# Sparse attention's first loads and query scaling placed in the selection stage, its first masks on VectorE, and the softmax combination of differential attention in pieces of 512 keys

## The reference

```
# sparse ("nsa") attention, 8 heads in 2 groups; compressed, selected and window branches
imp = where(forced, 1e9, p_cmp @ a_sel); _, idx = top_k(imp, 8)     # 8 blocks of 64 keys for each query and group
s = q . k_selected * scale ; p_sel = softmax(s - slope * dist)      # selected branch
s = q . k_window   * scale ; p_win = softmax(s - slope * dist)      # window branch, 512 keys
out = g0 * o_cmp + g1 * o_sel + g2 * o_win

# differential attention, 4 heads, two score maps each
p = softmax(q_c . k_c * scale - slope * dist)        # c = 0, 1; causal, up to 2048 keys
a = p[0] - lam * p[1]
out = a @ v
```

## Time and profile before

| | us |
|---|---|
| median of 3 runs | 3420.95 |
| lowest and highest | 3409.36, 3424.22 |
| the profiled execution's own time | 3418.37 |
| its span in the trace | 3416.6 |

### The profile page before, as it was taken

One profiled execution on the slowest core, in us unless ns is written; L12 is line 12 of the kernel. 1 busy time (PEld: TensorE's weight loads), 2 busy tenths in 40 slices (PEclk: granted clock), 3 DMA queues, 4 the chain that ended last, 5 costly groups with the idle time before them and its releaser, 6 DMA issues. The chain is left out here.

```text
span 3416.6 us, 37491 instructions
## 1 busy us (share of the span) xinstructions
PE 2990.3 (88%) x13210; PEld 1767.3 (52%) x13211; DVE 1345.3 (39%) x3149; ACT 1000.7 (29%) x2050; POOL 558.6 (16%) x568
## 2 busy tenths in 40 slices
PE   8999999999977758989999969999699899859990
PEld 5644444444446635555665646666544355547670
DVE  3421212111114545555565647777511111152236
ACT  1100000000005524545555536666411012113332
POOL 0121110111003330221222120000121100001116
PEclk9999999999988769999999979999899999969995
DMA  3211211121141220011111020110254333615848
GB/s 118 77 63 68 71 66 57 68 71 65 59 143 47 80 84 27 15 51 35 55 41 49 7 93 1 38 38 1 111 219 144 143 129 123 270 60 208 319 166 307
DMA packets 120754, 323.41 MB, mean 95 GB/s; under 512 B 13216, under 2 KB 49696, under 8 KB 112416
## 3 DMA queue, kind: packets, MB, share of 16 engines
q1 hardware_dynamic: 100320, 247.54, 20.5%
q0 software_dynamic: 14096, 51.39, 4.6%
q10 hardware_dynamic: 6192, 22.55, 1.6%
HBM read 206.42 MB, written 115.02 MB: 94 GB/s over the span
## 5 line engine op out<-in xcount | busy, mean ns | idle before, releaser
L305 PE MATMUL p_ps<-token_sums,p_ws 128*128 128x512 f32 x768 | 340.0, 592 | 0.0
L305 PEld LDWEIGHTS p_ps<-token_sums,p_ws 128*128 128x128 f32 x768 | 145.9, 190 | 183.8 <-issue 183.8
L305 PE MATMUL p_ps<-xnT,p_w 128*128 128x512 f32 x512 | 233.1, 598 | 5.2 <-PEq L59 5.2
L1683 PE MATMUL o_ps<-o_w,o_mT 128*128 128x512 f32 x512 | 224.2, 596 | 14.0 <-DMA o_w<-in_w_out 14.0
L314 ACT ACTIVATE p_kept<-p_ps 128x512 f32<-128x512 f32 x32 | 19.1, 598 | 737.4 <-PE p_ps L305 737.4
L1038 PE MATMUL b_po<-b_probT,vsw 128*64 128x256 f32 (+1 forms) x1824 | 231.1, 375 | 0.0
L1113 DVE CUSTOM_DVE_ANT_0 b_prob_s<-b_pq,b_sel 128x896 f32<-128x896 f32 (+5 forms) x192 | 167.8, 911 | 144.0 <-PE b_pq L997 124.4
L327 DVE TENSOR_TENSOR p_kept<-p_ps,p_kept 128x512 f32<-128x512 f32 x96 | 66.4, 692 | 391.6 <-PE p_ps L305 391.6
L1275 PE MATMUL d_pq<-d_keys,d_q 64*128 64x512 f32 (+3 forms) x640 | 177.7, 589 | 27.4 <-DVE d_seg_max L1381 15.1
L1381 DVE CUSTOM_DVE_ANT_0 d_prob<-d_pq,d_bias 128x1024 f32<-128x1024 f32 (+6 forms) x192 | 167.5, 910 | 72.7 <-PE d_pq L1275 70.2
L997 PE MATMUL b_pq<-ks,b_q 64*128 64x512 f32 (+3 forms) x688 | 166.0, 542 | 29.0 <-DVE b_seg_max L1113 16.1
(11 more groups left out here) (277 smaller groups left out, 4755.9 us busy)
## 6 DMA issues: line engine op xcount, KB each, us to landing
projT<-p_stage SPq DMA_DIRECT2D x128, 256.0 KB, 2.3
y<-e_y ACTq DMA_DIRECT2D x43, 512.0 KB, 4.3
p_w<-in_wt SPq DMA_DIRECT2D x16, 1024.0 KB, 5.5
gates_T<-projT SPq DMA_DIRECT2D x16, 1024.0 KB, 9.9
wgu<-in_w_gu SPq DMA_DIRECT2D x4, 4096.0 KB, 15.7
y<-m_zeros POOLq DMA_DIRECT2D x20, 512.0 KB, 11.8
p_xin<-in_x SPq DMA_DIRECT2D x16, 512.0 KB, 3.7
mergedT<-m_stage SPq DMA_DIRECT2D x8, 1024.0 KB, 11.4
```

Source lines behind the costliest of these rows:

```text
L305: mm = nc.tensor.matmul(ps[n % 8][:], weights[:, k, :], moving[:, k, :], start=(k == 0), stop=(k == HK - 1))
L1683: mm = nc.tensor.matmul(ps[b][k][:], mT[:, b, dt, :], w[:, dt, k * 512:(k + 1) * 512], start=(dt == 0), stop=(dt == DT - 1))
```

## The change

In the selection stage SyncE also issues, behind the store of `ya`, the query scales, queries and distances of pairs 0 and 1 and the window distances, and GpSimd scales the queries of pairs 0 and 1. The tiles for these move to a scope that begins before the compression stages. In sparse attention the masks of pair 0 are added by VectorE, at the head of its list, and those of pair 1 by GpSimd, at the head of its own. In differential attention `combine` issues one instruction for each chunk of up to 512 keys, and `turn` waits for its own chunk. Cut diff:

```diff
@@ selection
             sp.dma_start(d["ya"], s.ya[:]).then_inc(ya_out, 16)
+            sp.dma_start(s.b_qscale[:], d["nsa_qscale"]).then_inc(s.b_const_in, 16)
+            for k in range(2):
+                load_queries(sp, d, s, k)
+            for k in range(2):
+                load_distances(sp, d, s, k)
+            sp.dma_start(s.b_wdist[:], d["win_dist"]).then_inc(s.b_const_in, 16)
             sp.wait_ge(ya_out, 16)
+
+        @block.gpsimd
+        def _(pool):
+            pool.wait_ge(s.b_const_in, 32)
+            for k in range(2):
+                scale_queries(nc, pool, s, k)
+def load_queries(sp, d, s, k):
+    p = PAIR_ORDER[k]
+    sp.dma_start(s.b_q[k % 2][:], d["qkT"][0:PAIRS, :, p * 2 * P:(p + 1) * 2 * P].rearrange("i p c -> p i c")).then_inc(s.b_q_in[k % 2], 16)
+def load_distances(sp, d, s, k):
+    for j in range(2):
+        n = (2 * PAIR_ORDER[k] + j + 1) * P
+        for g in range(GROUPS):
+            sp.dma_start(s.b_sel[:, j, g, sel_at(k):sel_at(k) + n], d["dist"][:, T - n:T]).then_inc(s.b_dist_in[k % 2], 16)
+def scale_queries(nc, pool, s, k):
+    pool.wait_ge(s.b_q_in[k % 2], 16 * (k // 2 + 1))
+    for i in range(PAIRS):
+        x = s.b_q[k % 2][:, i, :]
+        nc.gpsimd.tensor_scalar(x, x, s.b_qscale[:, i:i + 1], None, mybir.AluOpType.mult).then_inc(s.b_q_ready, 1)
@@ sparse_attention
+        def mask_row(eng, op, k, j, g, done):
+            t = 2 * PAIR_ORDER[k] + j
+            n = 2 * (t + 1)
+            x = sel[:, j, g, sel_at(k):sel_at(k) + (t + 1) * P].rearrange("p (b c) -> p b c", c=SEL_BLOCK)
+            op(x, x, s.mask[:, g, t, 0:n].unsqueeze(2).to_broadcast([P, n, SEL_BLOCK]), ALU.add).then_inc(done, 1)
...
-            sp.dma_start(qscale[:], d["nsa_qscale"]).then_inc(const_in, 16)
-            sp.dma_start(wdist[:], d["win_dist"]).then_inc(const_in, 16)
             load(0)
             load(1)
...
-            pool.wait_ge(const_in, 32)
-            scale_queries(0)
-            mask(0)
             mask(1)
-            scale_queries(1)
             make_rates(0)
...
-            pe.wait_ge(const_in, 32)
...
-                    if branch == "S" and i == 0:
-                        dve.wait_ge(masked, 4 * (u // PAIRS + 1))
+                    if branch == "S" and u < PAIRS:
+                        dve.wait_ge(first_masked, 4)
+                    elif branch == "S" and i == 0:
+                        dve.wait_ge(masked, 4 * (u // PAIRS))
...
-            dve.wait_ge(const_in, 32)
+            dve.wait_ge(dist_in[0], 64)
+            for j in range(2):
+                for g in range(GROUPS):
+                    mask_row(dve, nc.vector.tensor_tensor, 0, j, g, first_masked)
+            dve.wait_ge(s.b_const_in, 32)
@@ differential_attention
-                if f == f_first[u]:
-                    pe.wait_ge(combined, u + 1)
+                pe.wait_ge(combined, f + 1)
...
-                        dve.wait_ge(combined, u - 2)
+                        dve.wait_ge(combined, f_end[u - 3])
...
-                nc.vector.scalar_tensor_tensor(out=prob[0][u % 4][:, 0:n], in0=prob[1][u % 3][:, 0:n], scalar=stat[:, u % RING, 6:7],
-                                               in1=prob[0][u % 4][:, 0:n], op0=ALU.mult, op1=ALU.add).then_inc(combined, 1)
+                for f in range(f_first[u], f_end[u]):
+                    cols = slice(flat[f][1], flat[f][1] + flat[f][2])
+                    nc.vector.scalar_tensor_tensor(out=prob[0][u % 4][:, cols], in0=prob[1][u % 3][:, cols], scalar=stat[:, u % RING, 6:7],
+                                                   in1=prob[0][u % 4][:, cols], op0=ALU.mult, op1=ALU.add).then_inc(combined, 1)
```

More of the change, by code:

```diff
@@ L722, in _, with sel_at @@
                 nc.vector.tensor_scalar(s.mask[:, g], imp[:, g], NEG, NEG, ALU.not_equal, ALU.mult)
+SELW = 20 * P
+def sel_at(k):
+    return 0 if k % 2 == 0 else SELW - (2 * PAIR_ORDER[k] + 2) * P
+def load_queries(sp, d, s, k):
[7 more added lines that the diff above has]
+def scale_queries(nc, pool, s, k):
+    from concourse import mybir
+    pool.wait_ge(s.b_q_in[k % 2], 16 * (k // 2 + 1))
+    for i in range(PAIRS):
+        x = s.b_q[k % 2][:, i, :]
+        nc.gpsimd.tensor_scalar(x, x, s.b_qscale[:, i:i + 1], None, mybir.AluOpType.mult).then_inc(s.b_q_ready, 1)
 def chunks_of(start, count):
@@ L852, in sparse_attention @@
         sb = lambda name, shape: ctx.enter_context(nc.sbuf_tensor("b_" + name, shape, fp32))
-        wdist = sb("wdist", [P, WINDOW + P])
-        q = [sb(f"q{b}", [P, PAIRS, 2 * P]) for b in range(2)]
-        qscale = sb("qscale", [P, PAIRS])
+        wdist, q, sel, dist_in, q_ready = s.b_wdist, s.b_q, s.b_sel, s.b_dist_in, s.b_q_ready
         ya = [sb(f"ya{b}", [P, 2, NSA_HEADS * HD]) for b in range(2)]
-        sel = sb("sel", [P, 2, GROUPS, SELW])
         prob_s = [sb(f"prob_s{k}", [P, GROUPS, T]) for k in range(4)]
@@ L899, in load @@
                     sp.wait_ge(q_ready, PAIRS * (k - 1))
-                sp.dma_start(q[b][:], d["qkT"][0:PAIRS, :, cols].rearrange("i p c -> p i c")).then_inc(q_in[b], 16)
-                if k >= 2:
+                    load_queries(sp, d, s, k)
                     sp.wait_ge(scaled, GROUPS * (last_seg[(last_unit[k - 2], "S")] + 1))
[L903 to L906, removed]
+                    load_distances(sp, d, s, k)
                 if k >= 2:
@@ L928, in _ @@
         def _(pool):
[L929 to L933, removed]
             def mask(k):
-                p, b = PAIR_ORDER[k], k % 2
-                pool.wait_ge(dist_in[b], 64 * (k // 2 + 1))
+                pool.wait_ge(dist_in[k % 2], 64 * (k // 2 + 1))
                 for j in range(2):
-                    t = 2 * p + j
-                    n = 2 * (t + 1)
                     for g in range(GROUPS):
-                        x = sel[:, j, g, room(k):room(k) + (t + 1) * P].rearrange("p (b c) -> p b c", c=SEL_BLOCK)
-                        nc.gpsimd.tensor_tensor(x, x, s.mask[:, g, t, 0:n].unsqueeze(2).to_broadcast([P, n, SEL_BLOCK]), ALU.add).then_inc(masked, 1)
+                        mask_row(pool, nc.gpsimd.tensor_tensor, k, j, g, masked)
             def make_rates(u):
@@ L2281, in program @@
                 s.gates = sb(nsa, "gates", [P, NT, 3 * NSA_HEADS])
+                s.b_q = [sb(nsa, f"b_q{b}", [P, PAIRS, 2 * P]) for b in range(2)]
+                s.b_sel = sb(nsa, "b_sel", [P, 2, GROUPS, SELW])
+                s.b_wdist = sb(nsa, "b_wdist", [P, WINDOW + P])
+                s.b_qscale = sb(nsa, "b_qscale", [P, PAIRS])
+                s.b_q_in = [nc.alloc_semaphore(f"b_q_in{b}") for b in range(2)]
+                s.b_dist_in = [nc.alloc_semaphore(f"b_dist_in{b}") for b in range(2)]
+                s.b_const_in, s.b_q_ready = nc.alloc_semaphore("b_const_in"), nc.alloc_semaphore("b_q_ready")
                 with ExitStack() as cmp:
```

18 lines of the change are left out of this document (5 added, 13 removed).

## The result

The changed kernel takes 3402.21 us (median of 17 runs, 3396.3 to 3409.95), the kernel before beside it 3420.95 (17 runs, 3409.36 to 3426.86). The ratio is 0.9945, 95% interval 0.9937 to 0.9953: 18.7 us faster, where 38 were forecast. Half of the forecast is missing, and it is missing in one place.

The account below looks back on a forecast made before the run. TensorE, busy 88% of the span, was taken as the bound, so its idle time counts. 3418.4 - 13.9 (opening) - 22.4 (differential attention) = 3382.1, stated as 3383 us; range for 8 in 10: 3367 to 3407.

Parts of the forecast that it names:

- First masks on VectorE: Start of sparse attention: VectorE's four masks take 1.2 us, first score at 1212.5 instead of 1216.74, 4.3 us gained.
- rival 1: Start of sparse attention: VectorE's and GpSimd's masks take turns; 3392.5 if VectorE begins, 3396 if GpSimd begins; chance 0.33.
- the opening: Selection and start of sparse attention: first score 4.3 us earlier and a 9.6 us wait gone, together 13.9 us.
- Loads and scaling: Selection: loads behind the store land at 1203.5, GpSimd scales until 1210.8, so sparse attention starts at 1211.1 instead of 1205.96.
- Pair 1's masks and the wait at the turn: Sparse attention: GpSimd's masks run 1211.1 to 1225.0, so TensorE's 9.62 us wait for unit 0's rates goes whole.
- Combination in pieces: Differential attention: earlier turns gain 17.4 us over four heads, 0.14 us per extra piece; 22.4 us with the clock.
- clock term: Differential attention: shorter TensorE idle times spare part of the loss to a lower clock, 5 us, bounded by 0 and 13.
- rival 2: Differential attention: TensorE arrives earlier only to wait for `scale`; gain some 3 us, time 3401.5; chance 0.12.
- rival 3: Differential attention: turns gain nothing, 96 extra pieces cost 0.219 us each on VectorE's path, 21 us longer, 3425.5; chance 0.05.

Follow-up runs that it names:

- constants early: The changed kernel with the window distances loaded ahead of the queries and distances instead of behind them; 3390.57 us, ratio 0.9915.
- GpSimd behind: The changed kernel with one wait more: GpSimd starts pair 1's masks only when VectorE's four are done; 3384.66 us, ratio 0.9893.
- The opening with both faults mended: The changed kernel with window distances loaded early and GpSimd's masks waiting for VectorE's four; 3380.63 us, ratio 0.9877.
- the opening alone: The changed kernel with the combination whole again, so only loads, query scaling and first masks are moved; 3423.89 us, ratio 1.0005.
- late turn: The changed kernel, pieces kept, but TensorE's first turn of a unit waits for its last piece; 3433.96 us, ratio 1.0034.
- two pieces: The changed kernel with each combination in at most two instructions, the first 512 keys and then the rest; 3399.9 us, ratio 0.9935.
- second pair first: The changed kernel with window distances loaded early, pair 1's distances loaded ahead of pair 0's, and no wait between the engines' masks; 3389.78 us, ratio 0.991.

## Why the prediction was half right

- **The step that failed is "First masks on VectorE"**, which took 1.2 us for the four masks. They took 14.46, because rival 1 held, in its second form: GpSimd first, one of its masks ahead of each of VectorE's. That form had the turn of the rates back at its old time and the opening giving nothing. It was priced at 3396 from the earlier trace rows, whose overlapping pairs showed each engine waiting for the other; the argument against it, that four short instructions without a wait among them would run in one go, is what the single masks above refute. Of the 16.5 us by which the first score came late (1229.00 for 1212.5) the turns are 13.3.
- **Loads and scaling.** The other 3.2: scaling began at 1206.82 for 1203.5, 0.9 of it because the whole execution was later there. The bytes were counted right, but the slow start of the loads was not hidden under the store: from 1188 to 1190, just behind it, the DMA moved 102 GB/s. SyncE took 10.72 us to issue the eight distance loads while the 4 MB store was under way, the load issued last, for which GpSimd waits, went out at 1191.70, and it took 15.0 us to land. With the constants early, GpSimd began at 1194.28 and the stage was 7.5 us shorter. The prediction noted that GpSimd waits for that load and never asked whether an order without the wait was at hand.
- **Pair 1's masks and the wait at the turn.** Right. From first score to turn it is 1245.22 - 1216.74 = 28.5 us before, 19.05 after and 19.07 with GpSimd behind: the 9.62 us wait is gone whole. The time does not show it, because the first score itself comes 12.3 us later.
- **The opening with both faults mended** gives 21.7 us in medians, for 13.9 forecast. In its trace the turn of the rates stands 51.1 us behind the selection's first load, for 70.1 before: 19.0 us, which is the forecast's 13.9 and the 5.1 by which GpSimd's scaling was to end the stage late and no longer does. The clock was rightly left out of the sum: full clock came 7.1 us behind the turn before and 2.3 behind it with GpSimd behind, and the rest of the stage took the same (755.3 and 755.7 us).
- **Combination in pieces.** Right in size: 25.1 us between the traces, 18.6 to 21.7 between medians, 22.4 forecast. The turns' wait went from 33.6 to 8.1. In the traces TensorE's idle time in the stage fell by 21.0 us (443.6 - 383.3 against 418.5 - 379.2) for the 17.4 forecast (which should read 4 x 4.3 = 17.2), and its busy time by 4.1 for the 5 of the clock term. The gains of single units were not checked one by one. A piece costs VectorE 0.13 us for the 0.14 forecast. By the prediction's working from the Trainium skill's "VectorE: DVE Perf Modes", section "The DRAIN you can't avoid", a piece would cost its whole fixed 0.219 us; the runs show 0.13, and 0.105 to 0.14 on the path. The Trainium skill excepts there a next instruction that is not held, so the 0.08 us of overlap in the earlier trace rows do not speak against it.
- **Rivals 2 and 3** fell: the wait for `scale` rose by 0.7 us only, and the pieces with their early turns made the stage shorter, not longer. That the measured 3402.21 lies next to rival 2's 3401.5, and inside the stated range, is chance: the range reached so far up because of rival 1. Rival 1's 3396 is the traced execution's time (3396.3); the median is 6 us above it.
- **Open:** the sizes of single opening edits in medians (17.5, 11.6, 21.6 us for GpSimd behind, constants early, both) differ from the shifts of the turn in one trace each, counted from the selection's first load (12.6, 20.8, 20.9), by up to 9 us, while the runs of one kernel spread by 4 to 19 us. Whether the turns occur in some executions of the kernel with constants early was not seen in a trace.

## What to carry to other kernels

Before work is moved to a second engine to run beside the first, look whether both forms of instruction meet in the trace: if a pair that overlaps shows one lasting as long as the other, the short list takes the pace of the long one, and one wait that lets the short list go first is worth more than the overlap. Ask also whether the move is needed at all: here one engine doing all the masks was only 0.7 us behind. Let what a consumer waits for be issued first, small loads above all, not behind a burst that the issuing queue itself is held up by. When a long instruction is cut so that its reader can start, try cutting off the first piece only: the reader may come late enough for the rest.

## What the hardware showed that was not expected

- GpSimd and VectorE sums of two SBUF tensors that are ready together go strictly in turns, one of each, 128 to 256 columns against 1920 to 2048: four VectorE masks that take 1.17 us alone took 14.46 us in the traces of all five kernels where both lists started together (the changed one, the opening alone, late turn, two pieces, second pair first), beside four GpSimd masks that took 14.19 for 13.92 alone. GpSimd, with the long ones, loses 0.27 us, VectorE 13.3.
- VectorE's score instruction, with one operand in PSUM, is not held: with GpSimd behind it takes 0.29 us at 1215.97, inside GpSimd's 13.92 us, as it does undisturbed in the earlier trace rows. The Trainium skill's "SBUF — State Buffer", section "SBUF: two separate sides", names the VectorE instruction with two SBUF inputs as the one that shares with GpSimd, and the trace agrees.
- SyncE can be the one that waits: the issue of a load takes 0.43 us in most rows, and eight took 10.72 us while the 4 MB store was under way, one of them 7.20 us; in the kernel before, with no store under way, the same eight took 4.8.
